# Fetching the weight panels of a two-block transformer kernel in pairs

## The reference

```
# first block
h = rmsnorm(x); z = h @ w_in + b_in                  # 1024 -> 2048 + 1280 + 1280 + 1024 + 1024
u = silu(layernorm(conv31(glu(z)))) ; y_a = u @ conv_w_out + b
y_b = (rg_lru(conv4(z_rx)) * gelu(z_rg)) @ lru_w_out
x = x + (sigmoid(z_ga) * y_a + sigmoid(z_gb) * y_b) @ w_mix_out
x = x + (silu(h @ ffn_w1) * (h @ ffn_w3)) @ ffn_w2   # h = rmsnorm(x), hidden 2816
x = rmsnorm(x)
# second block
mods = silu(c) @ w_ada + b_ada                       # one row of 1024 by 1024 x 9216
x = x + 0.5 * gt1 * rmsnorm(swiglu(h1, w_gu1, w_dn1))
x = x + gt2 * rmsnorm(token_mixer(h2, w_in, ...))    # gated linear attention + forgetting attention
x = x + 0.5 * gt3 * rmsnorm(swiglu(h3, w_gu2, w_dn2))
```

## Time and profile before

| | |
|---|---|
| median of three runs | 2584.41 us (2583.6 to 2585.2) |
| profiled execution | 2587.58 us |
| its span, first to last instruction | 2585.6 us |
| TensorE busy | 2408.6 us, 93% |
| VectorE / ScalarE / GpSimd busy | 985.8 / 932.8 / 1049.2 us |
| granted TensorE clock, mean | 0.941 |
| bytes moved | 267.85 MB, 104 GB/s over the span |

### The profile page before, as it was taken

One profiled execution on the slowest core, in us unless ns is written; L12 is line 12 of the kernel. 1 busy time (PEld: TensorE's weight loads), 2 busy tenths in 40 slices (PEclk: granted clock), 3 DMA queues, 4 the chain that ended last, 5 costly groups with the idle time before them and its releaser, 6 DMA issues.

```text
span 2585.6 us, 34308 instructions
## 1 busy us (share of the span) xinstructions
PE 2408.6 (93%) x10490; PEld 1936.3 (75%) x10490; DVE 985.8 (38%) x1696; ACT 932.8 (36%) x1628; POOL 1049.2 (41%) x796
## 2 busy tenths in 40 slices
PE   7999978988999998999997999998999997999997
PEld 6888856867787886888876777776666686788886
DVE  5699877246614314100114234444344222210012
ACT  4333374333322223333323433334343333443331
POOL 4455343544444443444453433332110244444443
PEclk9999998998999999999997999997897798999998
DMA  4334432446736432333331233333110332233331
GB/s 145 95 96 114 123 122 73 155 132 226 238 112 215 149 91 70 94 102 94 97 90 53 82 103 97 97 98 110 33 37 17 105 94 62 81 95 96 98 97 57
DMA packets 130409, 267.85 MB, mean 104 GB/s; under 512 B 14336, under 2 KB 14464, under 8 KB 129696
## 3 DMA queue, kind: packets, MB, share of 16 engines
q1 hardware_dynamic: 119520, 236.51, 31.1%
q10 hardware_dynamic: 10816, 30.38, 3.1%
HBM read 252.12 MB, written 14.68 MB: 103 GB/s over the span
## 4 chain that ended last, share of the span: by engine, by line
PE 69%; issue 14%; DVE 7%; POOL 5%; ACT 2%; DMA 2%; POOLq 0%; DVEq 0%; SPq 0%; ACTq 0%
PE bank L836 21%; PE bank L837 20%; PE bank L838 20%; POOL wlo L363 4%; DVE G L1251 2%; PE bank L1125 2%; DMA G<-d_ada 2%; PE bank L1153 2%; PE bank L1127 1%; PE bank L1139 1%; PE bank L941 1%; DVE G L1551 1%; DVE tmp L1459 1%; DVE G L1561 1%; PE bank L893 0%
## 5 line engine op out<-in xcount | busy, mean ns | idle before, releaser
L363 POOL TENSOR_TENSOR wlo<-raw,whi 128x512 fp32r<-128x512 f32 x750 | 995.0, 1333 | 1427.8 <-ACT whi L435 1427.1
L836 PE MATMUL bank<-a_hi,whi 128*128 128x512 f32 x1992 | 800.3, 402 | 21.1 <-POOL wlo L363 9.2
L838 PE MATMUL bank<-a_lo,whi 128*128 128x512 f32 x1992 | 787.2, 395 | 0.0
L837 PE MATMUL bank<-a_hi,wlo 128*128 128x512 f32 x1992 | 787.1, 395 | 0.0
L435 ACT ACTIVATE whi<-raw 128x512 fp32r<-128x512 f32 x750 | 466.6, 627 | 771.4 <-PE bank L838 647.6
L836 PEld LDWEIGHTS bank<-a_hi,whi 128*128 128x128 f32 x1992 | 380.6, 191 | 124.2 <-issue 23.7
L838 PEld LDWEIGHTS bank<-a_lo,whi 128*128 128x128 f32 x1992 | 381.0, 191 | 81.0
L837 PEld LDWEIGHTS bank<-a_hi,wlo 128*128 128x128 f32 x1992 | 381.6, 192 | 76.4 <-issue 0.5
L836 PE MATMUL bank<-b_hi,whi 128*128 128x512 f32 x788 | 313.4, 398 | 24.8 <-DVE G L1473 8.9
L837 PE MATMUL bank<-b_hi,wlo 128*128 128x512 f32 x788 | 311.1, 395 | 0.0
L838 PE MATMUL bank<-b_lo,whi 128*128 128x512 f32 x788 | 311.1, 395 | 0.0
(11 more groups left out here) (231 smaller groups left out, 1923.2 us busy)
## 6 DMA issues: line engine op xcount, KB each, us to landing
raw<-d_stream SPq DMA_DIRECT2D x750, 256.0 KB, 2.6
G<-d_ada SPq DMA_DIRECT2D x72, 512.0 KB, 4.1
spill_rv<-tmp ACTq DMA_DIRECT2D x32, 256.0 KB, 2.1
G<-spill_rv ACTq DMA_DIRECT2D x4, 1024.0 KB, 9.3
G<-spill_rv ACTq DMA_DIRECT2D x2, 2048.0 KB, 10.0
G<-d_x ACTq DMA_DIRECT2D x4, 512.0 KB, 5.4
spill_ga<-G ACTq DMA_DIRECT2D x8, 256.0 KB, 3.6
spill_gb<-G ACTq DMA_DIRECT2D x8, 256.0 KB, 3.5
```

What stands on the lines that cost most here:

```text
L363: pool.tensor_tensor(wlo[:, s % SRING, :], raw[:, s % RING, :], whi[:, s % SRING, :].bitcast(F32), ALU.subtract).then_inc(lo_done, 1)
L836: pe.matmul(out_ps, w_hi, hi[:, k, :], start=first and q == 0, stop=False)
L837: pe.matmul(out_ps, w_lo, hi[:, k, :], start=False, stop=False)
L838: mm = pe.matmul(out_ps, w_hi, lo[:, k, :], start=False, stop=last and q == len(ks) - 1)
```

## The change

Only even panels start a load. It waits until GpSimd is done with both slots, and fetches panels p and p+1, 512 KB, into slots p % 8 and p % 8 + 1. The semaphores `raw_landed` are now one for each pair of slots, and ScalarE waits for the pair before it splits either panel. In `ada_run` the w_ada loads keep their place: behind an even panel's step there is the pair's load ahead of one, behind an odd panel's step nothing.

```diff
-        raw_landed = [sem(f"raw_landed{i}") for i in range(RING)]
+        raw_landed = [sem(f"raw_landed{i}") for i in range(RING // 2)]
...
                 p = base + s
-                sp.wait_ge(lo_done, i * 8 + (p + 1))
-                src = stream[p] if isinstance(i, int) else stream[ds(i * 8 + p, 1)].rearrange("a p c -> p (a c)")
-                sp.dma_start(raw[:, p % RING, :], src).then_inc(raw_landed[p % RING], 16)
+                if p % 2:
+                    return
+                sp.wait_ge(lo_done, i * 8 + (p + 2))
+                src = stream[p:p + 2] if isinstance(i, int) else stream[ds(i * 8 + p, 2)]
+                sp.dma_start(raw[:, p % RING:p % RING + 2, :], src.rearrange("a p c -> p a c"))\
+                    .then_inc(raw_landed[p % RING // 2], 16)
...
-                act.wait_ge(raw_landed[p % RING], i * (16 * n // RING) + (p // RING + 1) * 16)
+                act.wait_ge(raw_landed[p % RING // 2], i * (16 * n // RING) + (p // RING + 1) * 16)
```

## The result

The changed kernel took 2593.94 us at the median of ten runs (2589.89 to 2601.59), the kernel before 2586.27 (2583.6 to 2590.45) in the same comparison: a ratio of 1.0033, 95% interval 1.0024 to 1.0042. A second comparison of the same two, on another occasion, gave 1.0023 (1.0014 to 1.0033). So it is slower by 6 to 9 us. The profiled execution has a span of 2591.3 us, 5.7 more than before.

A forecast was written before the change was run, and what follows sets the result against it. TensorE, busy 2408.6 of 2585.6 us, was taken to bound the kernel, so loads count only where it stands still. Terms 0 + 1.4 + 1.4 + 0.8 = +3.6 us gave 2588.0 us; own range 2585 to 2592.5, whole range 2582 to 2595.

The forecast's parts named there:

- slower rival: w_ada turns become bound by DMAs, each of nine losing about 1 us, plus longer sums: 12 us, 2596; chance 0.18.
- Nothing outside the w_ada stretch: Ring of panels outside w_ada: even panels requested one panel later, seven ahead of use, still hidden; cost 0.
- the beginning: Kernel start: the first matmul waits for VectorE's operand, not panels; cost 0, bounded at about 3 us.
- fewer load instructions at nothing: SP queue: 375 fewer DMAs of 0.33 us each give nothing, except in some w_ada turns.
- The pair lands like a w_ada piece: 512 KB panel load: 1.5 us fixed delay plus 1.9 us transfer, landing after 3.4 us.
- The gate moves the even pieces, and the slack ahead of L1262 shrinks: Ordinary w_ada turn: later pair wait delays pieces, piece 5 by 1.2 us; slack of 1.5 us shrinks to 0.3.
- Waits for pieces to some 70 us, halts 20 to 24 with the first near 7.8: Signs in w_ada turns: VectorE's idle time grows from 57 us to some 70; L941's nine waits sum to 20 to 24.
- The first turn +1.4: First w_ada turn: pair 2-3 waits for the burst's first low, pieces come later, TensorE waits: +1.4 us.
- The first of gu1b +0.8: First turn of gu1b, a middle case: piece 5 comes 0.7 us past its slack; +0.8 us, bounds 0 and +1.5.
- Seven ordinary turns +0.2 each: Ordinary w_ada turns: the slack is eaten, 0.2 us lost in each of seven; +1.4 us, bounds 0 and +4.6.
- The faster rival: Larger transfers bring odd pieces sooner, first w_ada turn's halt shrinks from 6.42 to 1.52 us: 6.5 us gained, 2578; chance 0.07.
- No effect at all: Transfers stay hidden, since pieces have slack and the pair moves the same bytes: 2584.4 to 2585 us; chance 0.18.

The follow-up runs named there:

- late gate elsewhere: Kernel before with single panels, even panels waiting for one more free slot everywhere except in the w_ada turns: ratio 0.9991 to the kernel before.
- late gate alone: Kernel before with single panels, even panels waiting for one more free panel only in the w_ada turns: ratio 1.0044 to the kernel before.
- four buffers: w_ada given four buffers in place of two; ratio to the kernel before 0.9993 in the changed kernel, 0.9987 in the kernel before with single panels.
- pairs again: Changed kernel measured once more with no edit: ratio 1.0023 to the kernel before.
- fours ahead of pieces 3 and 7: Changed kernel with four panels (1 MB) per load, placed in the w_ada turns ahead of pieces 3 and 7: ratio 1.0056 to the kernel before.
- single panels behind the pieces: Kernel before with each single panel's load in the w_ada turns moved behind the piece after its old place: ratio 0.9988 to the kernel before.
- first of the fours: Changed kernel with four panels (1 MB) per load and one wait for four slots, order in the w_ada turns kept: ratio 1.0316 to the kernel before.
- pairs one step later: Changed kernel with the pair's load in the w_ada turns moved one step later, ahead of the odd piece: ratio 1.0006 to the kernel before.

## Why the prediction was right or wrong

The time lies in the range (2594 against 2582 to 2595), and the direction and place are those of the forecast; the likeliest outcome by its chances, no more than 0.2% of change, is not what came. The ratio of 1.0023 to 1.0033 is beyond 0.2%, to which I had given 0.33. The forecast's own size was +3.6 us; 6 to 9 us came. As a difference that is still about in its own range of +0.5 to +8; as a time it isn't, since that range ended at 2592.5 us and the kernel before, too, was 2 us slower in this comparison than the 2584.41 that I had started from. That 2594 lies in the whole range is owed to the room that was left for the slower rival.

- *Nothing outside the w_ada stretch; the beginning; fewer load instructions at nothing.* Right: two waits for the ring, 0.9 us, and no loss with the late gate elsewhere. The rest of the span is not the same to a microsecond, as I had asked, but 3.6 us shorter, within what it varies by (7 us over all profiles).
- *The pair lands like a w_ada piece.* Right: 3.5 us at the median, 3.4 taken. The fit of the Trainium skill beside which I had put this ("DMA: Bandwidth & Descriptors", Anatomy of one DMA; an estimate of 3.2 us) was measured on loads issued from GpSimd, and these are issued from SP.
- *The gate moves the even pieces, and the slack ahead of L1262 shrinks.* Right, and shown by the late gate alone. In the third turn the steps, moved by the 1.8 us, say piece 5 done at 636.6; it was 635.7. The slack left was 1.14 us, where I had 0.3. The queue of 1.9 us for an item was too dear in that turn. The panels' waits on SP fell from 76 to 48, not to half.
- *Waits for pieces to some 70 us, halts 20 to 24 with the first near 7.8.* 73.8; 24.1; 8.36.
- *The first turn +1.4.* +1.94. *The first of gu1b +0.8.* +1.20.
- *Seven ordinary turns +0.2 each, 1.4 together, bounds 0 and 4.6.* This is the term that was mis-sized: they gave 4.5. The bound was also wrong in itself: eight items of 2.04 us from 621.5 end at 637.8 and not 637.95, which makes the turn 0.5 us longer and the bound 3.6, and 4.5 is beyond it. I had put only lateness into the term, and at one clock. Three of the seven are as before; the fifth turn has 0.74, which is 2.38 us more halt at a clock that saved 1.64. The 3.8 us of the second, the sixth and the second of gu1b lie in turns with the usual halt of 1.5 us and a mean clock of 0.86 to 0.88, each behind a halt that was longer than usual. I had priced a long sum (1.63 us, from the earlier trace rows) and then used it only for the slower rival; a turn at a higher or a lower clock had no term. That the long halt is the cause is argued by place and not shown by a run.
- *No row for the down product.* It is 1.61 us longer. That isn't shown to be the gate's: the clock fell there, and it did so in kernels that lose nothing as well.
- *The slower rival*, all nine turns bound by DMAs at about 1 us each, did not come: turns 3, 4 and the last are unchanged to 0.01 us. Its price for the clock was the part that was wanted. *The faster rival* failed by the gate, as argued: the first halt grew. *No effect at all* is what the pairs give once no piece stands behind their wait, or with four buffers. The rule of the Trainium skill that I had weighed ("DMA: Bandwidth & Descriptors", Bandwidth: batch to 1 MiB or more) has no gain here at any size tried; that fits, with nothing that waited for panels.

Sum by my terms against the stretch: lateness 1.94 + 0.74 + 1.20 = 3.9 us, where the forecast had 3.6; turns at a lower clock 3.8; down product 1.6. By what was measured: halts +5.5 (first turn 1.94, fifth 2.38, first of gu1b 1.19) and TensorE's work +3.8 (5.4 in the three turns and the down product, less 1.6 in the fifth). In the other kernels that work took 404.7 to 406.8 us in the stretch where the loss was small or gone, 408.0 to 408.6 in the pairs again, the late gate alone and the fours ahead of pieces 3 and 7. So the mechanism of the forecast, pieces held behind the pair's wait, was right, and near its size; that the loss is 6 to 9 us and not about 4 is owed to a second one, in TensorE's clock, that it had no term for.

## What to carry to other kernels

When transfers on one queue are merged, the merged one waits for the last of its slots, and all that stands behind it on the queue waits too, whether or not it has to do with the ring. Look for the stream that has only two buffers and stands behind the merged wait; move the load behind that stream's, or give the stream more buffers, before asking for larger transfers. Where no engine waits for the ring in the profile, as here, there is nothing for larger transfers to give: none of the kernels with 512 KB or 1 MB was faster, beyond the intervals, than its counterpart with single panels. And a longer halt may cost more than its length: here 5.5 us of halts went with 3.8 us more of TensorE's work.

## What the runs showed of the hardware that was not expected

Where TensorE's clock falls moves between kernels that differ only in load order. The down product's beginning, from 723 to 740 us, in the kernel before and in the one with single panels behind the pieces:

```profile
723.00:740.00 17.00, 17.00 (x84) 14.33 (x85) 2.12 (x4) 4.31 (x7) 7.23 (x6) 1.00 0.30 91
```

```profile
723.00:740.00 17.00, 17.00 (x71) 13.98 (x71) 1.46 (x3) 3.82 (x7) 6.93 (x6) 0.90 0.25 69
```

The second, at a mean clock of 0.90, pays about 1.6 us there (69.0 us in place of 67.4) and had gained as much in its fifth turn:

```profile
669.19:694.54 25.35, 23.84 (x112) 19.73 (x112) 15.26 (x13) 9.76 (x14) 11.69 (x8) 1.00 0.74 248
```

Whole turns that end with the usual halt of 1.5 us are of three kinds, in all kernels but the first of the fours, where no halt was that short: 25.4 us at a mean clock of 1.00, 27.0 at 0.94, and 28.4 to 29.5 at 0.85 to 0.89. Halts of 3.9 us and more were followed in all kernels by sums of 2.96 to 3.58 us instead of 1.95. Between 1.5 and 2.8 us the same halt was followed by either: 2.63 by a sum of 1.95 and a turn of 26.95 us (pairs one step later), 2.71 by 2.96 and a turn of 28.57 (the changed kernel), and 1.51 by 2.31 and a turn of 28.56 (the late gate elsewhere). What decides there stays open. A difference of 2 or 3 us between single profiles of two such kernels says nothing of the edit by itself.
